# Weights in two transfers of 1 MB a unit, with a semaphore for each, in a two-layer decoder trunk on one core

## The reference

```python
for l in range(DEPTH):                                   # DEPTH = 2
    h = rms_norm(x, norm_mix[l]); proj = h @ w_in[l]     # 1024 x 3584
    ...                                                  # gated recurrence, dilated attention
    x = x + concat([y_hg, y_att]) @ w_out[l]
    x = x + memory_cross_attention(rms_norm(x), rms_norm(mem), wq_x[l], wkv_x[l], wo_x[l])
    x = x + hierarchical_moe(rms_norm(x), ...)
return rms_norm(x, norm_final)

def hierarchical_moe(h, w_rg, w_re, w_gate, w_up, w_down):
    # a softmax picks one of 4 groups, a top-2 in it picks 2 of its 4 experts: gates (n, 16)
    hg = einsum('nd,edf->nef', t, w_gate)                # 16 experts, 1024 x 512
    hu = einsum('nd,edf->nef', t, w_up)
    act = silu(hg) * hu * gates[..., None]
    return einsum('nef,efd->nd', act, w_down)            # 16 experts, 512 x 1024
```

## Time and profile before

| | us |
|---|---|
| median of 3 runs | 1102.59 |
| lowest and highest of them | 1098.84, 1102.71 |
| the profiled execution's own time | 1101.56 |
| its span, first to last instruction | 1099.7 |
| TensorE busy in the span | 1031.4 (94%) |
| packets of SP's queue, share of 16 DMA engines' span | 59.7% |

### The profile page before, as it was taken

One profiled execution on the slowest core, in us unless ns is written; L12 is line 12 of the kernel. 1 busy time (PEld: TensorE's weight loads), 2 busy tenths in 40 slices (PEclk: granted clock), 3 DMA queues, 4 the chain that ended last, 5 costly groups with the idle time before them and its releaser, 6 DMA issues.

```text
span 1099.7 us, 10478 instructions
## 1 busy us (share of the span) xinstructions
PE 1031.4 (94%) x4366; PEld 556.3 (51%) x4366; DVE 397.3 (36%) x722; ACT 136.8 (12%) x303; POOL 58.0 (5%) x105
## 2 busy tenths in 40 slices
PE   6999999999997999999998999999998699999995
PEld 5757556567564443333333855565864333333332
DVE  5203455622143233232233315662032443334332
ACT  3010001312010111100111000041011011111011
POOL 3001111000010000000000012100000100000000
PEclk9999999999999999999999999999999799999998
DMA  8954334154047999999989542325363499999992
GB/s 343 428 234 153 105 125 153 31 204 153 1 169 271 392 417 426 411 427 411 421 369 425 211 153 91 139 80 192 116 228 153 158 430 425 427 428 426 428 427 100
DMA packets 25239, 293.54 MB, mean 267 GB/s; under 512 B 3296, under 2 KB 3552, under 8 KB 8544
## 3 DMA queue, kind: packets, MB, share of 16 engines
q1 hardware_dynamic: 19392, 266.40, 59.7%
q10 hardware_dynamic: 4640, 22.19, 5.2%
q0 software_dynamic: 1152, 4.19, 1.0%
HBM read 283.33 MB, written 9.44 MB: 266 GB/s over the span
## 4 chain that ended last, share of the span: by engine, by line
PE 86%; DMA 7%; DVE 4%; issue 1%; ACT 1%; DVEq 0%; SPq 0%; POOL 0%; ACTq 0%
PE bank L816 18%; PE bank L487 12%; PE bank L635 10%; PE bank L840 9%; PE bank L495 9%; DMA ring<-in_w_experts 5%; PE bank L506 5%; PE bank L508 5%; PE bank L846 5%; PE bank L564 3%; PE bank L477 2%; PE bank L687 1%; PE bank L700 1%; PE bank L716 1%; DVE hT L1291 1%
## 5 line engine op out<-in xcount | busy, mean ns | idle before, releaser
L816 PE MATMUL bank<-ring,hT 128*64 128x512 f32 x816 | 209.9, 594 | 4.1 <-DMA late<-in_w_experts 1.8
L487 PE MATMUL bank<-ring,hT 128*128 128x512 f32 x320 | 140.3, 592 | 0.0
L816 PEld LDWEIGHTS bank<-ring,hT 128*64 128x64 f32 x816 | 66.9, 137 | 113.9 <-issue 112.9
L635 PE MATMUL bank<-ring,hT 128*128 128x512 f32 x256 | 112.1, 594 | 0.0
L495 PE MATMUL bank<-hT,ring 128*128 128x256 f32 x448 | 99.1, 384 | 2.0 <-DVE hT L1291 2.0
L1572 DVE TENSOR_TENSOR x<-bank,x 128x512 f32<-128x512 f32 x64 | 44.3, 692 | 137.6 <-PE bank L846 137.6
L487 PEld LDWEIGHTS bank<-ring,hT 128*128 128x128 f32 x320 | 59.6, 190 | 68.0 <-issue 67.9
L495 PEld LDWEIGHTS bank<-hT,ring 128*128 128x128 f32 x448 | 85.9, 193 | 14.5 <-DVE hT L1291 2.7
L635 PEld LDWEIGHTS bank<-ring,hT 128*128 128x128 f32 x256 | 48.0, 190 | 57.7 <-issue 56.8
L840 PE MATMUL bank<-ring,Vx 128*64 128x512 f32 x208 | 58.3, 613 | 3.4 <-ACT Vx L1049 1.5
L846 PE MATMUL bank<-PT 128*128 128x512 f32 x128 | 59.2, 605 | 0.0
(11 more groups left out here) (249 smaller groups left out, 1110.6 us busy)
## 6 DMA issues: line engine op xcount, KB each, us to landing
ring<-in_w_experts SPq DMA_DIRECT2D x80, 2048.0 KB, 15.2
ring<-in_w_mix SPq DMA_DIRECT2D x30, 2048.0 KB, 8.8
late<-in_w_experts SPq DMA_DIRECT2D x6, 2048.0 KB, 21.3
keys<-in_w_experts SPq DMA_DIRECT2D x5, 2048.0 KB, 20.7
work<-in_w_experts SPq DMA_DIRECT2D x5, 2048.0 KB, 25.2
late<-in_w_mix ACTq DMA_DIRECT2D x4, 2048.0 KB, 12.0
rot<-by_slot ACTq DMA_DIRECT2D x14, 512.0 KB, 10.3
by_slot<-late ACTq DMA_DIRECT2D x1, 4096.0 KB, 49.0
```

The source lines that it names most:

```text
L487: last = nc.tensor.matmul(b[:, :], lhs[:, c, m * P:(m + 1) * P], w[:, c, :], start=(c == 0), stop=(c == C - 1))
L635: last = nc.tensor.matmul(held[name[1:], n, m][:, :], hT[:, c, m * P:(m + 1) * P], w[:, c, :], start=(c == 0), stop=(c == C - 1))
L816: last = nc.tensor.matmul(banks[2 + g][b2 * CAP:(b2 + 1) * CAP, :], rowsT[p % 2][:, c, b2 * CAP:(b2 + 1) * CAP], w, start=(c == 0), stop=( ...
```

## The change

Each unit is loaded by two transfers of 1 MB, the first 2048 and the last 2048 floats of every partition, so 8 KB a partition each. Each slot has two semaphores, one for each half. SP waits once for a slot and issues both halves one after the other. `wait_unit` waits for both halves at once, as does `fill` without a half (the path for all experts on all tokens uses it so). In `routed`, the gate and up products wait for a unit's first half ahead of chunk 0 and for its second half ahead of chunk 4; the down products wait for the first half ahead of chunk 0 and for the second half ahead of chunk 2 of output half 0. Slots are freed as before, both halves together. The transfers on ACT's queue are unchanged.

```diff
-        loaded = [sem(f"loaded{s}") for s in range(SLOTS + len(LAST_SLOTS))]
+        loaded = [[sem(f"loaded{s}_{half}") for half in range(2)] for s in range(SLOTS + len(LAST_SLOTS))]
...
-        def wait_loaded(eng, L, key):
+        def wait_loaded(eng, L, key, half):
             slot, nth, _ = PLACES[L, key]
-            eng.wait_ge(loaded[slot], 16 * nth)
+            eng.wait_ge(loaded[slot][half], 16 * nth)
...
+            def load(slot, src):
+                n = C * W // 2
+                for half in range(2):
+                    sp.dma_start(slot_view(slot)[:, half * n:(half + 1) * n], src[:, half * n:(half + 1) * n]).then_inc(loaded[slot][half], 16)
...
-                    sp.dma_start(slot_view(slot), w_mix[L, u, :, :]).then_inc(loaded[slot], 16)
+                    load(slot, w_mix[L, u, :, :])
...
-                        sp.dma_start(slot_view(slot), w_experts[s // 2, N_EXPERTS * L + 2 * p + s % 2, :, :]).then_inc(loaded[slot], 16)
+                        load(slot, w_experts[s // 2, N_EXPERTS * L + 2 * p + s % 2, :, :])
...
             def wait_unit(L, name):
-                wait_loaded(pe, L, name)
+                for half in range(2):
+                    wait_loaded(pe, L, name, half)
...
-                def fill(p, s):
-                    wait_loaded(pe, L, (p, s))
+                def fill(p, s, half=None):
+                    for i in range(2) if half is None else (half,):
+                        wait_loaded(pe, L, (p, s), i)
...
                     for g in range(2):
-                        for b2 in range(2):
-                            fill(p, 2 * g + b2)
                         for c in range(C):
                             for b2 in range(2):
+                                if c % 4 == 0:
+                                    fill(p, 2 * g + b2, c // 4)
...
                     pe.wait_ge(r_evac[L], 4 * p + 2)
-                    for b2 in range(2):
-                        fill(p, 4 + b2)
                     for n in range(2):
                         for c in range(4):
                             for b2 in range(2):
+                                if n == 0 and c % 2 == 0:
+                                    fill(p, 4 + b2, c // 2)
```

## The result

The changed kernel takes 1095.51 us (median of 6 runs, 1092.67 to 1096.67) against 1102.65 us for the kernel before (6 runs, 1098.84 to 1104.13). The ratio is 0.9937 [0.9918, 0.9957]: 0.6% faster, and outside the predicted range. The profiled execution took 1096.6 us, with a span of 1094.8 us against 1099.7 us.

A forecast was written before the change was run, and what follows sets the result against it. The last load's landing in layer 1, behind a full DMA queue, was taken to set the end. Terms +0.7 (tail with half clock) and +0.1 (start) gave +0.8 us, so 1103.4 us, range 1099.5 to 1109.5.

The forecast's parts named there:

- Elsewhere: Start and layer 0: +0.1 us at the start, later loads hidden, TensorE's 6 more waits a pair cost nothing.
- the 0.03 for what I had not seen: Chance of 0.03 left for an outcome that neither the forecast nor any named rival covers.
- Price of a packet: Layer 1's load train: 8 KB packets take 314 ns, 0.08 us more a unit, last landing 3.1 us later.
- Dear packets: Rival, layer 1's loads: 8 KB packets move at the 4 KB rate, +5 to +7, about 1109 us; chance 0.13.
- free packets: Rival, last down products: first half there before TensorE, end 0.4 to 2.1 us earlier, about 1101 us; chance 0.09.
- a constant for each transfer: Rival, full load queue: 2.8 us paid 39 more times, +109, about 1212 us; chance 0.02.
- What the halves give back: Last down products: 8 of 32 instructions start on first halves, end 0.3 us earlier at full clock.
- The clock: Last down products: half clock from 1077.6 to 1081.0 us keeps its place, making the end +0.7 us.
- The start and layer 0: Start +0.1 us, second unit landing at 25.5 us but hidden; layer 0's K/V waits still absent.
- The sum: Whole kernel: +0.7 + 0.1 = +0.8 us, median 1103.4 us; chance 0.67.

The follow-up runs named there:

- experiment 1: Kernel before, no halves, with never-run instructions moving TensorE's routed path by 42 (layer 0) and 69 (layer 1), as the change does: 1095.31 us, ratio 0.9947.
- experiment 2: Changed kernel with 214 never-run instructions in layer 0, its routed path 256 instructions (one block) behind its place before the change: 1102.37 us, ratio 1.0005.
- experiment 3: Kernel before with each unit loaded in two halves on one semaphore, both waited for together, TensorE's code unmoved: 1103.27 us, ratio 1.0024.
- experiment 8: Kernel before with the two paths swapped on every engine, so the routed path is fallen into and the other jumped to: 1098.04 us, ratio 0.997.
- experiment 6: Kernel before with TensorE's routed code of layer 0 moved by 224 never-run instructions: 1102.83 us, ratio 1.0001.
- experiment 5: Kernel before with TensorE's routed code of layer 0 moved by 18 never-run instructions: 1094.82 us, ratio 0.9942.
- experiment 7: Kernel before with TensorE's routed code of layer 0 moved by 162 never-run instructions: 1094.55 us, ratio 0.9933.
- experiment 12: Repeat of experiment 1, the kernel before with only its code moved, on the same chip as the changed kernel: 1095.43 us, ratio 0.9928.
- experiment 10: Kernel before with code moved, only the last two units halved, layer 1's routed path first, VectorE's last signal ahead of the exit jump: 1090.57 us, ratio 0.9892.

## Why the prediction was wrong

The step that failed stands under "Elsewhere": "TensorE gets 6 more waits a pair [...] A wait already met costs nothing". The sentence holds for the time in which a wait runs, and the earlier trace rows show it. But I priced only that, not the place that the added instructions give to everything behind them. In its place the runs show a stall of 4.2 us with 1.7 us more in the products behind it, nearly all from half clock, present or absent by where TensorE's routed path stands in a block of 256 instructions. Experiments 1 and 2 move the median by 6.3 and back. The stall stood in the chain and in TensorE's waits of the kernel before, as 4.17 us of "issue" in L794. A pause that no semaphore and no DMA explains was the thing to ask about, since any added instruction could move it. I took it as fixed, and put it into no row, no rival and no chance but the 0.03 for what I had not seen.

Point by point:

- **Price of a packet: right.** In 880 to 1040 us the changed kernel's queue of SP moves 64.65 MB with a share of 0.970 of 16 engines, which makes 315 ns for 8 KB, where 314 was forecast. The train is 2.6 us longer in the changed kernel and 2.9 in experiment 3, against 3.1 forecast. By an estimate from the Trainium skill's overhead per packet ("DMA: Bandwidth & Descriptors", section Why small descriptors are slow) it would have been 1.1, and the runs speak for the rows. Dear packets, free packets and a constant for each transfer (+109) are excluded by the same two trains.
- **What the halves give back: right.** The last landing was 2.48 us behind its first half by the step of the landings (2.49 forecast), and TensorE began before it. 10 instructions ran ahead of the second wait, not 8. Forecast was an end 0.3 us earlier in sum, without half clock. Counted from the train's first issue to the end of the down products, the changed kernel's two traces took 209.4 us, without half clock there. The kernel before took 210.3, with 1.7 of half clock in it; experiment 8, with the transfers of the kernel before and no half clock there, took 208.6. At equal clock the halves thus cost 0.8 us: they give back most of what the smaller packets cost, but not all.
- **The clock: kept where it had left.** The +0.7 us did not come: in both traces of the changed kernel the half clock is absent from the last products, worth 1.7 us. The premise that TensorE waits as much as before fell too: 0.5 us ahead of the up products, not 1.83. But the half clock is no effect shown to be the halves': it fell on pair 7's up products (L816) in experiments 1 and 6 (8.80 us against 7.10), on its down products in 5, 7 and 12, and on neither in the others. What sets its place in the tail was not tried.
- **The start and layer 0: right.** The first long run of products starts at 13.42 us, 0.08 later than in the earlier trace rows; no other load is waited for up to the end of layer 0's experts, so the K/V waits stayed absent. The second unit's second half landed at 24.1 us and not at the forecast 25.5; nothing waited for it either way. That run of products took 30.05 us against 30.89, which no experiment explains.
- **The sum** of these terms, +0.8 us, is nearest to experiment 3, the kernel in which TensorE's code did not move: +2.6 us [1.0, 4.3]. It lacked the 6 us that the code's place was worth.

The Trainium skill ("Runtime: NRT & Kernel Launch", section Instruction fetch mechanics) says that instructions are fetched in blocks of 16 KiB, 256 instructions, and that a taken branch to a block not present waits for its fetch. The trace agrees, with packets of 16384 B and 3.5 to 4.8 us for TensorE's taken branch into the routed path. It calls the cost of crossing a border mostly hidden. Just behind a taken jump it was 4.2 to 6.9 us here, in four kernels, and the measurement decides.

## What to carry to other kernels

Look for "issue" pauses of some microseconds in the chain of waits behind a jump, and ask of every edit how many instructions it adds ahead of them, even ones that never run. Before crediting a change of a few tenths of a per cent to its mechanism, time the kernel before with its code moved by as many instructions, and the changed one with its code moved back. A step where the rows were read rightly (packets, landings, waits already met) can still be beside the point when the pause that moves the time is somewhere else.

## What the runs showed of the hardware

- A taken compare and branch into the routed path took 3.5 to 4.8 us on TensorE, and a pause of 2.8 to 4.0 us stood behind VectorE's at the entry of layer 1; falling through took 0.09 us on TensorE (experiments 8 and 10).
- Behind the jump, the block after the first came 4.4 to 8.7 us later. Borders 15 and 47 instructions ahead cost 4.2 to 6.9 us; at borders 109 and more ahead there was no stall.
- TensorE's granted clock fell to 0.50 during such a stall or at its end in each of the four kernels that had one, and in none of the others at this place. In the products of L794 alone up to 2.7 us came on top (25 of them in 5.7 us, against 3.0 as 25/32 of the 3.83 at full clock).
- With smaller packets on one queue the other's transfers landed sooner: beside 8 KB packets on SP's queue, the next pair's rows on ACT's landed in 7.9 us (median of 14) instead of 10.3, and the zeroing of `by_slot` in 33.0 us instead of 49.0. That fits a sharing packet by packet, as the earlier trace rows suggest.
